# A conv and attention trunk in split fp32: z projected last, products of one width, LayerNorm's channel sums on VectorE

## The chip, the cores and the metric

The kernel runs on one core of a Trainium2 chip. The metric is device time in microseconds. Three runs of the kernel before took 1514.84, 1517.45 and 1518.55 us: median 1517.45 us.

## The reference

The input x has 256 rows (positions) of 2048 channels, all in float32. Two layers follow each other.

Layer 0: `proj = rmsnorm(x) @ w_in` gives three parts a, b, z of 2048 channels each. `u = a * sigmoid(b)`. A causal depthwise convolution of 31 taps over the positions gives c. `cn` is LayerNorm of c over the channels. `y = silu(cn) * silu(z)`, and `x += y @ w_out`.

Layer 1: keys and values of three dilation groups from one normed x, queries of the three groups and a gate z from another, 16 heads of 128 channels. Attention with a relative bias, one softmax over the three groups of a head, times `silu(z)`, then `x += y @ w_out`, and a final RMSNorm.

## The kernel before, in words

**Split products.** Every float32 operand is kept as two float32r parts: hi (rounded) and lo (what is left). A product is hi*hi + hi*lo + lo*hi. Activations lie transposed in `act_a[:, kt, part, :]` (K tile kt of 16, part 0 is hi, 1 is lo, 256 positions). A weight *slab* is 1 MB: 16 K tiles by 128 output columns. SyncE loads it into a ring `raw` (`load_slab`), ScalarE rounds its two halves to `w_hi` (`split_hi`, L257), GpSimd (conv and both output projections) or VectorE (attention) subtracts to get `w_lo` (`split_lo`, L266), and TensorE multiplies (`project`, L280 and L282). In `project` the w_hi tile is multiplied with 512 columns, both parts of the activation side by side, so the bank of PSUM gets hi*hi in its lower and hi*lo in its upper 256 columns; w_lo with part 0 adds 256 columns to the lower ones. To get the result, ScalarE copies the upper half to SBUF (`copy_upper`, L481; `copy_upper_head`, L579) and VectorE adds the lower half (`add_halves`, L712; `head_sum`, L870).

**Conv stage.** One loop over 16 channel tiles; per tile three slabs a, b, z (`CONV`, three raw buffers, six half-slab buffers). VectorE makes u (`glu`, L747), the z gate (L752), and the 31 taps of the tile before (`tap`, L722 to L728, accumulators in PSUM bank 3, two chains joined at L735). All engines run fixed programs in order; semaphores tie them.

**LayerNorm.** When all taps are done, TensorE multiplies a constant 1/2048 matrix with the 16 tiles of `conv` (mean, L1045), VectorE subtracts it (L792), ScalarE squares (L514), TensorE does 16 products again (variance, L1051), ScalarE takes the root (L517), VectorE the reciprocal (L795). Then for each tile: VectorE scales (L802), ScalarE silu with gain and bias (L523), VectorE times the gate (L806), ScalarE rounds to hi (L528), VectorE subtracts to lo (L810). The first product of `a_w_out` (`out_project`, L300 to L302) waits for the lo of tile 0.

**After it.** Four column chunks of `a_w_out` in four slabs each; RMSNorm, transposes, the two inputs of layer 1 (`kv_input`, `q_input`); 16 heads of ten slabs, with the scores, softmax and attention of the head before put between slabs; `b_w_out`; the final norm.

The relative bias rows are made by three products (L1034) after the first three slabs, copied to SBUF (L760) and stored to DRAM by SyncE after the loads of the conv stage.

Of the kernel before, what the change touches and what calls it, by code (L numbers as in the profile page):

```python
# [30 lines left out]
P = 128  # L31
S = 256
# [61 lines left out]
Y_LOOP_SPLITS = {10: (2, (0,)), 13: (2, (1,))}  # L94
LATE_Q_INPUT = {2: range(4, 8), 3: range(8, 12), 4: range(12, KT)}

CONV = Stream(0, 3 * KT, 3, 3, 6, 0)
A_OUT = Stream(3 * KT, CHUNKS * KT // RKT, KT // RKT, 4, 4, 6 * KT)
# [4 lines left out]
def fills(stream, slot):  # L103

    n = 0
    for s in (CONV, A_OUT, QKV, B_OUT):
# [12 lines left out]
def build(nc, x, a_norm, a_w_in, a_conv_w, a_conv_b, a_ln_g, a_ln_b, a_w_out, kv_norm, w_kv, b_norm,  # L119
          b_w_in, b_w_out, rel_bias, final_norm, bucket_rows, out):  # L120
    ctx = ExitStack()
    with ctx:
# [8 lines left out]
        def sem(name):  # L131
# [9 lines left out]
        taps = sb("taps", [P, TAP_ROWS + 1])  # L141
# [12 lines left out]
        upper = sb("upper", [P, 3, S])  # L154

        xn, u, a_sum, b_sum, b_sig, z_sum, z_sig, odd_taps, ln_std, ln_rstd = shared(
            ("xn", [P, TT, D], F32), ("u", [P, TAPS - 1 + S], F32), ("a_sum", [P, S], F32),
            ("b_sum", [P, S], F32), ("b_sig", [P, S], F32), ("z_sum", [P, S], F32),
            ("z_sig", [P, S], F32), ("odd_taps", [P, S], F32), ("ln_std", [P, S], F32),
            ("ln_rstd", [P, S], F32))  # L160
# [18 lines left out]
        bias_vec = raw[0:HEADS, 1, 0:NG * BIAS_W]  # L179
# [17 lines left out]
        upper_copied, summed = sem("upper_copied"), sem("summed")  # L197
        b_gated, z_gated, gate_ready = sem("b_gated"), sem("z_gated"), sem("gate_ready")
        u_ready, taps_copied, tap_done = sem("u_ready"), sem("taps_copied"), sem("tap_done")
        mean_ready, centered, squared, var_part = sem("mean_ready"), sem("centered"), sem("squared"), sem("var_part")  # L200
# [33 lines left out]
        def load_slab(sp, stream, turn, j, src):  # L234

            slot = stream.slot(j)
            if isinstance(turn, int) and turn == 0 and j < stream.ring:
                before = {id(CONV): None, id(A_OUT): CONV, id(QKV): A_OUT, id(B_OUT): QKV}[id(stream)]
# [31 lines left out]
        def project(pe, stream, turn, j, dst, source, source_ready=None):  # L270


            for half in (2 * j, 2 * j + 1):
                slot = stream.half_slot(half)
                pe.wait_ge(lo_dve if stream is QKV else lo_pool, stream.lo_halves(turn, half))
                for k in range(KT // 2):
                    kt = (half % 2) * (KT // 2) + k
                    if source_ready is not None:
                        pe.wait_ge(source_ready, kt + 1)
                    nc.tensor.matmul(dst[:, 0:2 * S], w_hi[:, slot, k * P:(k + 1) * P],  # L280
                                     source[:, kt, :, :], start=(kt == 0), stop=False)
                    mm = nc.tensor.matmul(dst[:, 0:S], w_lo[:, slot, k * P:(k + 1) * P],  # L282
                                          source[:, kt, 0, :], start=False, stop=(kt == KT - 1))
# [67 lines left out]
        def _(sp):  # L351
# [6 lines left out]
            for j in range(3):  # L358
                load_slab(sp, CONV, 0, j, w_in_cols[:, :, j * D:j * D + P])
# [3 lines left out]
            with sp.Fori(1, KT) as c:  # L363
                cols = [sp.snap(c * P + j * D) for j in range(3)]
                for j in range(3):
                    load_slab(sp, CONV, c, j, w_in_cols[:, :, bass.ds(cols[j], P)])

            sp.wait_ge(vec_copied, NG)
            sp.dma_start(bias_dram.ap(), bias_vec).then_inc(vec_stored, 16)
            sp.wait_ge(vec_stored, 16)  # L370
# [51 lines left out]
        def _(pool):  # L422
# [8 lines left out]
            with pool.Fori(0, KT) as c:  # L431
                for j in range(3):
                    split_lo(pool, CONV, c, j, lo_pool)
# [9 lines left out]
        def _(act):  # L443
# [17 lines left out]
            split_hi(act, CONV, 0, 0)  # L461
            act.wait_ge(param_ready, 2)
            for kt in range(KT):
# [5 lines left out]
                if kt in (9, 13):  # L469
                    split_hi(act, CONV, 0, 1, halves=((kt - 9) // 4,))  # L470


            def copy_upper(c, j):


                act.wait_ge(mm_done, CONV.mm_halves(c, 2 * j + 1))
                if j == 0:
                    positive(act, summed, 3 * c - 2)
                else:
                    act.wait_ge(summed, 3 * c + 1)  # L480
                nc.scalar.activation(upper[:, j, :], bank[j][:, S:2 * S], ACT.Copy).then_inc(upper_copied, 1)  # L481
# [710 lines left out]
```

## Time and profile before

The profiled execution took 1517.13 us, its span 1515.3 us.

| | before |
|---|---|
| median of 3 runs | 1517.45 us |
| profiled execution, and its span | 1517.13 us, 1515.3 us |
| TensorE busy | 1462.7 us (97%) |
| VectorE busy | 861.6 us (57%) |
| ScalarE busy | 704.0 us (46%) |
| GpSimd busy | 386.9 us (26%) |

The span starts with the first instruction and ends with the last one. A busy share over the whole span mixes stages; the rows further down are read stage by stage. Starts are in us from the span's start. The time of one instruction of a pipelined engine is longer than the distance to the next one's start; where instructions follow each other it is the distance of the starts that counts.

### The profile page before, as it was taken

The numbers are of one execution on the slowest core, as the hardware profiler recorded it, in microseconds if no ns is written. First come the engines' busy times: TensorE is split into PE (matmuls) and PEld (weight loads), VectorE is DVE, ScalarE is ACT, GpSimd is POOL, SyncE is SP. The second block draws the span as 40 slices with busy tenths as digits, with TensorE's granted clock in tenths as the row PEclk, the third lists the DMA queues.
The fourth block names the chain that finished last, engine by engine and source line by source line (L and its number), as shares of the span: only waits on it lengthen the run. The fifth ranks groups of instructions, "written<-read, shape, count | busy, mean of one in ns | idle before, by whom it ended". The sixth has DMA issues, their size and how long they took to land.

```text
span 1515.3 us, 23156 instructions
## 1 busy us (share of the span) xinstructions
PE 1462.7 (97%) x8198; PEld 1272.7 (84%) x8198; DVE 861.6 (57%) x1433; ACT 704.0 (46%) x1036; POOL 386.9 (26%) x168
## 2 busy tenths in 40 slices
PE   6999999969989999999999999999999999999997
PEld 5888888747868888888888888888888888888786
DVE  3798998971175554555555555555555554554333
ACT  6444444355454444444444444454444444544543
POOL 4888888608800000000000000000000000000595
PEclk9999999979999999999999999999999999999999
DMA  8666666505569656666566666665666656653652
GB/s 224 195 187 187 190 194 192 198 1 173 160 197 255 180 167 179 191 177 177 166 183 184 179 176 172 180 189 162 186 177 180 188 157 186 180 165 118 250 195 83
DMA packets 454127, 268.32 MB, mean 177 GB/s; under 512 B 4353, under 2 KB 436481, under 8 KB 453426
## 3 DMA queue, kind: packets, MB, share of 16 engines
q1 hardware_dynamic: 454098, 267.99, 61.4%
q8 instruction: 14, 0.23, 0.1%
q14 instruction: 9, 0.07, 0.0%
q10 hardware_dynamic: 6, 0.02, 0.0%
HBM read 263.71 MB, written 4.29 MB: 177 GB/s over the span
## 4 chain that ended last, share of the span: by engine, by line
issue 77%; POOL 15%; PE 6%; ACT 1%; DMA 1%; POOLq 0%; DVE 0%; SPq 0%; ACTq 0%
POOL w_lo L266 15%; PE bank L301 2%; PE bank L300 2%; PE bank L302 2%; DMA param_rows<-a_ln_b_dram 1%; ACT act_a L466 0%; ACT w_hi L257 0%; PE bank L1016 0%; POOLq L265 0%; PE bank L1007 0%; SPq L356 0%; ACT bank L654 0%; DVE y L972 0%; POOLq L431 0%; DVE resid L956 0%
## 5 line engine op out<-in xcount | busy, mean ns | idle before, releaser
L280 PE MATMUL bank<-act_a,w_hi 128*128 128x512 f32 x2304 | 807.4, 394 | 6.2 <-DVE k_t L870 3.1
L266 POOL TENSOR_TENSOR w_lo<-raw,w_hi 128x1024 fp32r<-128x1024 f32 x160 | 386.0, 2434 | 1111.9 <-ACT w_hi L257 1111.8
L282 PE MATMUL bank<-act_a,w_lo 128*128 128x256 f32 x2304 | 645.3, 280 | 0.0
L257 ACT ACTIVATE w_hi<-raw 128x1024 fp32r<-128x1024 f32 x480 | 501.7, 1060 | 295.2 <-PE bank L282 217.6
L266 DVE TENSOR_TENSOR w_lo<-raw,w_hi 128x1024 fp32r<-128x1024 f32 x320 | 390.6, 1229 | 281.0 <-ACT w_hi L257 278.5
L280 PEld LDWEIGHTS bank<-act_a,w_hi 128*128 128x128 f32 x2304 | 434.0, 188 | 103.2 <-DVE k_t L870 3.4
L282 PEld LDWEIGHTS bank<-act_a,w_lo 128*128 128x128 f32 x2304 | 434.0, 188 | 0.0
L280 PE MATMUL bank<-act_b,w_hi 128*128 128x512 f32 x1024 | 357.8, 393 | 0.0
L282 PE MATMUL bank<-act_b,w_lo 128*128 128x256 f32 x1024 | 286.3, 280 | 0.0
L280 PEld LDWEIGHTS bank<-act_b,w_hi 128*128 128x128 f32 x1024 | 192.3, 188 | 41.9
L282 PEld LDWEIGHTS bank<-act_b,w_lo 128*128 128x128 f32 x1024 | 192.3, 188 | 0.0
L579 ACT ACTIVATE upper<-bank 128x256 f32<-128x256 f32 x160 | 61.5, 385 | 276.0 <-PE bank L282 276.0
L728 DVE SCALAR_TENSOR_TENSOR bank<-u,taps,bank 128x256 f32<-128x256 f32 x448 | 179.8, 486 | 0.0
L300 PE MATMUL bank<-w_hi,act_a 128*128 128x512 f32 x240 | 96.4, 402 | 7.8 <-DVE act_a L810 5.0
L301 PE MATMUL bank<-w_lo,act_a 128*128 128x512 f32 x240 | 95.6, 398 | 0.0
L302 PE MATMUL bank<-w_hi,act_a 128*128 128x512 f32 x240 | 95.1, 396 | 0.0
L481 ACT ACTIVATE upper<-bank 128x256 f32<-128x256 f32 x48 | 18.5, 386 | 99.2 <-PE bank L282 99.2
L300 PEld LDWEIGHTS bank<-w_hi,act_a 128*128 128x128 f32 x240 | 45.6, 190 | 20.2 <-issue 5.4
L870 DVE TENSOR_TENSOR k_t<-bank,upper 128x256 f32<-128x256 f32 x48 | 20.4, 424 | 62.9 <-PE bank L1080 37.9
L302 PEld LDWEIGHTS bank<-w_hi,act_a 128*128 128x128 f32 x240 | 45.5, 190 | 11.3
L301 PEld LDWEIGHTS bank<-w_lo,act_a 128*128 128x128 f32 x240 | 45.5, 190 | 10.6
L870 DVE TENSOR_TENSOR q_t<-bank,upper 128x256 f32<-128x256 f32 x48 | 20.4, 425 | 49.5 <-ACT upper L579 49.5
(119 smaller groups left out, 717.3 us busy)
## 6 DMA issues: line engine op xcount, KB each, us to landing
raw<-w_kv_dram SPq DMA_DIRECT2D x96, 1024.0 KB, 6.0
raw<-b_w_in_dram SPq DMA_DIRECT2D x64, 1024.0 KB, 6.6
raw<-a_w_in_dram SPq DMA_DIRECT2D x48, 1024.0 KB, 5.8
raw<-a_w_out_dram SPq DMA_DIRECT2D x16, 1024.0 KB, 5.0
raw<-b_w_out_dram SPq DMA_DIRECT2D x16, 1024.0 KB, 5.1
bias<-bias_dram SPq DMA_DIRECT2D x16, 384.0 KB, 8.1
x_sb<-x_dram SPq DMA_DIRECT2D x2, 1024.0 KB, 7.4
resid_dram<-x_sb SPq DMA_DIRECT2D x1, 2048.0 KB, 8.6
```

What stands on the lines that cost most here:

```text
L257: nc.scalar.activation(w_hi[:, stream.half_slot(half), :], raw[:, slot, part:part + HALF], ACT.Copy).then_inc(hi_done, 1)
L266: eng.tensor_tensor(w_lo[:, stream.half_slot(half), :], raw[:, slot, part:part + HALF], w_hi[:, stream.half_slot(half), :].bitcast(F32), A ...
L280: nc.tensor.matmul(dst[:, 0:2 * S], w_hi[:, slot, k * P:(k + 1) * P], source[:, kt, :, :], start=(kt == 0), stop=False)
L282: mm = nc.tensor.matmul(dst[:, 0:S], w_lo[:, slot, k * P:(k + 1) * P], source[:, kt, 0, :], start=False, stop=(kt == KT - 1))
L300: nc.tensor.matmul(banks[t][:, :], y_h, wide_hi, start=(kt == 0), stop=False)
L301: nc.tensor.matmul(banks[t][:, :], y_h, wide_lo, start=False, stop=False)
L302: mm = nc.tensor.matmul(banks[t][:, :], y_l, wide_hi, start=False, stop=(kt == KT - 1))
L481: nc.scalar.activation(upper[:, j, :], bank[j][:, S:2 * S], ACT.Copy).then_inc(upper_copied, 1)
L579: nc.scalar.activation(upper[:, j % 2, :], bank[j % 2][:, S:2 * S], ACT.Copy).then_inc(upper_copied, 1)
L728: nc.vector.scalar_tensor_tensor(out=odd_taps[:, :] if k == TAPS - 2 else acc, in0=u[:, k:k + S], scalar=taps[:, tap_row(k):tap_row(k) + 1 ...
L870: nc.vector.tensor_tensor(dst, bank[j % 2][:, 0:S], upper[:, j % 2, :], ALU.add).then_inc(summed, 1)
```

## The change

- All a and b slabs are projected first: a loop of 8 turns with two tiles each (`AB`, four raw buffers, four half-slab buffers, PSUM banks 0 to 3), then the 16 z slabs (`ZS`, written out, not a loop).
- `project` has three products of 256 columns that all add to the lower 256 columns of the bank: w_hi with part 0, w_hi with part 1, w_lo with part 0. No copy of the upper half and no sum: the sigmoid of b, the silu of z (ScalarE, one `Silu` in place of sigmoid and product) and GLU read PSUM. In the attention part ScalarE copies the 256 columns to k_t, v_t, q_t, z_t (`copy_head`).
- `u` is a ring of four tiles. VectorE's taps run as one sequence of 496: after GLU of tile c it goes on up to tap 26*(c+1), and does the rest after the last GLU. The accumulators move to bank 4, the taps' factors are read from `param` directly.
- After each fourth tile VectorE adds four tiles of `conv` into `ch_sum`; TensorE makes the mean from four products in place of 16, put behind z slab 8. The squares come on ScalarE behind the split of z slab 12, VectorE sums them in fours, the variance product stands behind z slab 11, the root behind the split of slab 14. The reciprocal lies in PSUM. VectorE scales four tiles at a time; all 16 silus come on ScalarE ahead of the first split of `a_w_out`. Then the y products, and the hi and lo parts.
- The bias rows' products come after the first slab, SyncE stores them behind the first four z loads; they lie in `gate`.

```diff
-                    nc.tensor.matmul(dst[:, 0:2 * S], w_hi[:, slot, k * P:(k + 1) * P],
-                                     source[:, kt, :, :], start=(kt == 0), stop=False)
-                    mm = nc.tensor.matmul(dst[:, 0:S], w_lo[:, slot, k * P:(k + 1) * P],
-                                          source[:, kt, 0, :], start=False, stop=(kt == KT - 1))
+                    wide_hi = w_hi[:, slot, k * P:(k + 1) * P]
+                    wide_lo = w_lo[:, slot, k * P:(k + 1) * P]
+                    nc.tensor.matmul(dst[:, 0:S], wide_hi, source[:, kt, 0, :], start=(kt == 0), stop=False)
+                    nc.tensor.matmul(dst[:, 0:S], wide_hi, source[:, kt, 1, :], start=False, stop=False)
+                    mm = nc.tensor.matmul(dst[:, 0:S], wide_lo, source[:, kt, 0, :],
+                                          start=False, stop=(kt == KT - 1))
...
 # ScalarE
+            def gate_b(turn, n):
+                act.wait_ge(mm_done, AB.mm_halves(turn, 4 * n + 3))
+                positive(act, u_ready, 2 * turn + n - 1)
+                nc.scalar.activation(b_sig[:, n, :], bank[2 * n + 1][:, 0:S], ACT.Sigmoid).then_inc(b_gated, 1)
+            with act.Fori(2, KT // 2) as i:
+                for j in range(4):
+                    split_hi(act, AB, i, j)
+                    if j % 2 == 0:
+                        gate_b(i - 1, j // 2)
+            for n in range(KT):
+                split_hi(act, ZS, n // 4, n % 4)
+                if n in (0, 2):
+                    gate_b(KT // 2 - 1, n // 2)
+                if n >= 3:
+                    gate_z(n - 3)
+                if n == SQUARE_SLOT:
+                    for q in range(4):
+                        act.wait_ge(centered, q + 1)
+                        nc.scalar.activation(squares[:, q, :, :], conv[:, 4 * q:4 * q + 4, :],
+                                             ACT.Square).then_inc(squared, 1)
+                if n == STD_SLOT:
+                    act.wait_ge(var_ready, 1)
+                    nc.scalar.activation(ln_std[:, :], bank[7][:, 0:S], ACT.Sqrt,
+                                         bias=eps).then_inc(ln_std_ready, 1)
+            for kt in range(KT):
+                act.wait_ge(ln_scaled, kt // 4 + 1)
+                nc.scalar.activation(conv[:, kt, :], conv[:, kt, :], ACT.Silu, ...)
             split_hi(act, A_OUT, 0, 0)
+            gate_z(KT - 3)
             split_hi(act, A_OUT, 0, 1)
+            gate_z(KT - 2)
+            for kt in range(KT):
+                if kt == 0:
+                    act.wait_ge(mm_done, ZS.mm_halves(KT // 4 - 1, 7))
+                if kt == 2:
+                    gate_z(KT - 1)
+                act.wait_ge(y_ready, kt + 1)
+                nc.scalar.activation(act_a[:, kt, 0, :], conv[:, kt, :], ACT.Copy).then_inc(y_hi, 1)
                 if kt in Y_LOOP_SPLITS:                       # {7: (2, (0,)), 14: (2, (1,))}
                     split_hi(act, A_OUT, 0, *Y_LOOP_SPLITS[kt])
...
 # VectorE
+            for c in range(KT):
+                glu(c)
+                taps_up_to(min((c + 1) * PAIR_TAPS, (c + 1) * TAPS))      # PAIR_TAPS = 26
+            taps_up_to(KT * TAPS)
+            (centring by the mean, four pieces)
+            for q in range(4):
+                dve.wait_ge(squared, q + 1)
+                nc.vector.tensor_reduce(ch_sum[:, q, :], squares[:, q, :, :].rearrange("p k s -> p s k"),
+                                        AX.X, ALU.add).then_inc(sq_summed, 1)
+            (reciprocal, scaling in four pieces)
+            for kt in range(KT - 1):
+                gated_y(kt)
+            for kt in range(KT):
+                dve.wait_ge(y_hi, kt + 1)
+                nc.vector.tensor_tensor(act_a[:, kt, 1, :], conv[:, kt, :], act_a[:, kt, 0, :].bitcast(F32),
+                                        ALU.subtract).then_inc(y_lo, 1)
+                if kt == 4:
+                    gated_y(KT - 1)
...
 # TensorE
+            with pe.Fori(1, KT // 2) as i:
+                for j in range(4):
+                    pe.wait_ge(b_gated if j % 2 else u_ready, 2 * i + (j // 2 - 1))
+                    project(pe, AB, i, j, bank[j], act_a)
+            for n in range(KT):
+                if n < 4:
+                    pe.wait_ge(b_gated if n % 2 else u_ready, KT + (n // 2 - 1))
+                else:
+                    pe.wait_ge(gate_ready, n - 3)
+                project(pe, ZS, n // 4, n % 4, bank[n % 4], act_a)
+                if n == MEAN_SLAB:                            # 8
+                    pe.wait_ge(vec_copied, NG)
+                    for q in range(4):
+                        pe.wait_ge(ch_summed, q + 1)
+                        mm = nc.tensor.matmul(bank[6][:, 0:S], mean_w[:, :], ch_sum[:, q, :], start=(q == 0), stop=(q == 3))
+                    mm.then_inc(mean_ready, 1)
+                if n == VAR_SLAB:                             # 11
+                    for q in range(4):
+                        pe.wait_ge(sq_summed, q + 1)
+                        mm = nc.tensor.matmul(bank[7][:, 0:S], mean_w[:, :], ch_sum[:, q, :], start=(q == 0), stop=(q == 3))
+                    mm.then_inc(var_ready, 1)
...
 # attention, ScalarE (VectorE's head_sum is gone)
+            def copy_head(h, j):
+                dst = [k_t, v_t, q_t][j // NG][:, j % NG, :] if j < 3 * NG else z_t[:, :]
                 act.wait_ge(mm_done, QKV.mm_halves(h, 2 * j + 1))
+                if j == 3 * NG:
+                    act.wait_ge(z_gate_ready, h + 1)
+                nc.scalar.activation(dst, bank[j % 2][:, 0:S], ACT.Copy).then_inc(head_copied, 1)
```

## Rows read from the trace of the kernel before

**Rows 1.** The page: TensorE's busy time, the granted clock in 40 slices, ScalarE's splits.

```profile
PE 1462.7 (97%) x8198; PEld 1272.7 (84%) x8198; DVE 861.6 (57%) x1433; ACT 704.0 (46%) x1036; POOL 386.9 (26%) x168
...
PEclk9999999979999999999999999999999999999999
...
L257 ACT ACTIVATE w_hi<-raw 128x1024 fp32r<-128x1024 f32 x480 | 501.7, 1060 | 295.2 <-PE bank L282 217.6
```

**Rows 2.** A stretch of the attention part: length, busy us by engine, clock.

```profile
600.00:800.00 200.00, 200.00 (x1176) 176.99 (x1175) 107.47 (x133) 90.39 (x129) 0.00 (x0) 1.00 0.63 177
```

**Rows 3.** Timeline of TensorE around LayerNorm: start, us, idle before it.

```profile
296.51 6.74 PE L1045 MATMUL bank<-conv,mean_w 128*128 128x256 f32 x30 [3.56 <-DVE conv L735]
...
328.37 0.77 PE L300 MATMUL bank<-w_hi,act_a 128*128 128x512 f32 x1 [5.00 <-DVE act_a L810]
```

**Rows 4.** Groups of instructions by form: busy us, mean ns, idle before, releasers.

```profile
L300 PE MATMUL bank<-w_hi,act_a 128*128 128x512 f32 x240 | 96.4, 402 | 7.8 <-DVE act_a L810 5.0 <-POOL w_lo L266 2.7
...
L889 DVE TENSOR_REDUCE stat<-prob 128x1 f32<-128x768 f32 x16 | 15.2, 947 | 0.0
```

**Rows 5.** Timelines of ScalarE, VectorE, TensorE at the third attention slab.

```profile
445.33 0.39 ACT L579 ACTIVATE upper<-bank 128x256 f32<-128x256 f32 x1
...
446.93 0.42 DVE L870 TENSOR_TENSOR k_t<-bank,upper 128x256 f32<-128x256 f32 x1
...
447.41 0.50 PE L280 MATMUL bank<-act_a,w_hi 128*128 128x512 f32 x1 [3.06 <-DVE k_t L870]
```

**Rows 6.** Timeline of TensorE: the fourth conv slab's start, and two attention pairs.

```profile
43.09 0.50 PE L280 MATMUL bank<-act_a,w_hi 128*128 128x512 f32 x1
...
700.42 0.39 PE L280 MATMUL bank<-act_a,w_hi 128*128 128x512 f32 x1
700.65 0.28 PE L282 MATMUL bank<-act_a,w_lo 128*128 128x256 f32 x1
700.77 0.39 PE L280 MATMUL bank<-act_a,w_hi 128*128 128x512 f32 x1
```

**Rows 7.** Timeline of TensorE: six fp32 products of 256 columns, six of 128.

```profile
1432.31 1.46 PE L1107 MATMUL bank<-prob_t,v_rows 128*128 128x256 f32 x6
1433.60 0.83 PE L1109 MATMUL bank<-prob_t,v_rows 128*128 128x128 f32 x6
```

**Rows 8.** Timeline of VectorE over one tile of taps.

```profile
150.16 0.55 DVE L722 TENSOR_SCALAR bank<-u,taps 128x256 f32<-128x256 f32 x1
...
156.49 0.41 DVE L712 TENSOR_TENSOR b_sum<-bank,upper 128x256 f32<-128x256 f32 x1
156.82 5.18 DVE L728 SCALAR_TENSOR_TENSOR bank<-u,taps,bank 128x256 f32<-128x256 f32 x13
...
163.37 0.62 DVE L747 TENSOR_TENSOR u<-a_sum,b_sig 128x256 f32<-128x256 f32 x1
163.91 0.41 DVE L712 TENSOR_TENSOR z_sum<-bank,upper 128x256 f32<-128x256 f32 x1
```

**Rows 9.** Timeline of TensorE after that hole: first and last slow wide product.

```profile
448.69 0.63 PE L280 MATMUL bank<-act_a,w_hi 128*128 128x512 f32 x1
...
451.25 0.63 PE L280 MATMUL bank<-act_a,w_hi 128*128 128x512 f32 x1
```

**Rows 10.** Timelines of VectorE and ScalarE in LayerNorm.

```profile
311.44 4.62 DVE L792 TENSOR_TENSOR conv<-conv,bank 128x1024 f32<-128x1024 f32 x4 [0.98 <-PE bank L1045]
...
323.92 1.75 DVE L795 RECIPROCAL ln_rstd<-ln_std 128x256 f32<-128x256 f32 x1 [7.86 <-ACT ln_std L517]
...
312.70 4.45 ACT L514 ACTIVATE xn<-conv 128x1024 f32<-128x1024 f32 x4 [14.99 <-DVE conv L792]
...
323.90 1.28 ACT L523 ACT_TABLE_LOAD   x1
326.16 1.09 ACT L523 ACTIVATE conv<-conv,param 128x256 f32<-128x256 f32 x2 [0.98 <-DVE conv L802]
```

**Rows 11.** Timelines of VectorE (alone, and beside POOL) and of POOL.

```profile
326.80 0.42 DVE L806 TENSOR_TENSOR conv<-conv,gate 128x256 f32<-128x256 f32 x1 [0.33 <-ACT conv L523]
...
338.03 2.24 DVE L806 TENSOR_TENSOR conv<-conv,gate 128x256 f32<-128x256 f32 x1 [0.40 <-ACT conv L523]
...
337.58 2.41 POOL L266 TENSOR_TENSOR w_lo<-raw,w_hi 128x1024 fp32r<-128x1024 f32 x1 [41.11 <-ACT w_hi L257]
```

More of the change, by code:

```diff
@@ L781, in _ @@
-            last = KT - 1
-            load_taps(last, param[:, last, 0:TAP_ROWS + 1])
-            for k in range(TAPS):
-                tap(last, k)
-            join_taps(last, conv[:, last, :])
-            gate_out(last, gate[:, last, :])
+            done_taps = [0]
+            for c in range(KT):
+                glu(c)
+                taps_up_to(min((c + 1) * PAIR_TAPS, (c + 1) * TAPS))
+            taps_up_to(KT * TAPS)
             dve.wait_ge(mean_ready, 1)
             for q in range(4):
-                mean = bank[4][:, 0:S].unsqueeze(1).to_broadcast([P, 4, S])
+                mean = bank[6][:, 0:S].unsqueeze(1).to_broadcast([P, 4, S])
@@ L1025, in _ @@
             pe.wait_ge(in_lo, 2)
-            for j in range(3):
+            for j in range(4):
                 if j == 1:
                     pe.wait_ge(in_lo, KT)
-                project(pe, CONV, 0, j, bank[j], act_a, in_lo if j == 0 else None)
-            pe.wait_ge(bias_in, 32)
-            pe.wait_ge(rel_mask, 1)
-            for g in range(NG):
-                nc.tensor.matmul(bank[5 + g][0:HEADS, :], rel, buckets[:, g * BIAS_W:(g + 1) * BIAS_W],
-                                 start=True, stop=True).then_inc(vec_made, 1)
@@ L1036, in _ @@
-            with pe.Fori(1, KT) as c:
-                for j in range(3):
-                    pe.wait_ge(summed, 3 * c + (j - 2))
-                    project(pe, CONV, c, j, bank[j], act_a)
-            for kt in range(KT):
-                if kt in (0, KT - 1):
-                    pe.wait_ge(tap_done, (TAPS + 1) * (KT - 1 if kt == 0 else KT))
-                mm = nc.tensor.matmul(bank[4][:, 0:S], mean_w[:, :], conv[:, kt, :], start=(kt == 0),
-                                      stop=(kt == KT - 1))
@@ L1047, in _ @@
-            mm.then_inc(mean_ready, 1)
-            for q in range(4):
-                pe.wait_ge(squared, q + 1)
-                for k in range(4):
-                    mm = nc.tensor.matmul(bank[5][:, 0:S], mean_w[:, :], squares[:, q, k, :],
-                                          start=(q + k == 0), stop=(q + k == 6))
-                mm.then_inc(var_part, 1)
+                project(pe, AB, 0, j, bank[j], act_a, in_lo if j == 0 else None)
+                if j == 0:
+                    pe.wait_ge(bias_in, 32)
+                    pe.wait_ge(rel_mask, 1)
+                    pe.wait_ge(in_lo, KT)
+                    for g in range(NG):
+                        if g == 2:
+                            pe.wait_ge(vec_copied, 1)
+                        nc.tensor.matmul(bank[6 + g % 2][0:HEADS, :], rel, buckets[:, g * BIAS_W:(g + 1) * BIAS_W],
+                                         start=True, stop=True).then_inc(vec_made, 1)
```

263 lines of the change are left out of this document (106 added, 157 removed).

## The prediction

> **What bounds the kernel now.** I read the page's busy table and clock line first, then the grouped instructions, then single stretches. TensorE is busy for 97% of the span and its granted clock stands at the upper level except in slices 8 and 9 [rows 1], so the time is the number of columns that it streams plus the holes. In the attention part one slab (16 K tiles of w_hi over 512 columns, w_lo over 256) follows the other with no hole: 200.00 us busy in 200 us [rows 2]. There only the price of the products counts, and an edit on VectorE or ScalarE is worth nothing. The large hole is LayerNorm's: the last conv product ends at 296.51 - 3.56 = 292.95 us (so it starts 0.28 before, and a next one could follow at 292.8), the first product of a_w_out starts at 328.37 [rows 3], 35.6 us later. In between come the taps of the last tile, two sums by ones-matmuls, the centring, squares, root, and the first y. Smaller holes: 2.7 us that products of a_w_out wait for POOL [rows 4], and 3.06 us at the third attention slab, for a sum on VectorE that stands behind its own split and its q inputs [rows 5].
>
> **The product split in three (every slab of a, b, z, q, k, v).** Per K tile 512+256 columns become 256+256+256: the same 768 columns, one matmul and one weight load more. Between starts, the 512-column product takes 230 ns (700.42 to 700.65) and the 256-column one about 120 ns by the two decimals of the rows [rows 6]. More exactly: from 43.09 to 292.8 us run 45 slabs of 16 pairs [rows 3, 6], 5.55 us a slab, 346.8 ns a pair, so 230 + 116.8. Three narrow ones at 116.8 are 350.4 ns: +3.6 ns a K tile, 5.61 us a slab. Does the extra load fit? The load for the next wide product already hides in the 117 ns window, and six fp32 products with a load each follow one another at (0.83 - 0.275)/5 = 111 ns [rows 7]. Lower end: cost goes by columns alone, 347, nothing added. Upper end: the fp32 256-column product, 216 ns ((1.46 - 0.38)/5) [rows 7], which is another data type and far off; I take 353 as the upper end I believe. Accumulating into columns used 117 ns before is not new, the wide product does so now.
> The attention part has 160 slabs, 2560 K tiles, all on the path: 2560 x 3.6 = **+9.2 us** (0 to +16). The same toll of 768 x 3.6 = 2.8 us in the conv part is inside the times below.
> The Trainium skill, "TensorE: Matmul & The Clock Gate" (Wait — 56ns, not 53.3ns?), has a fixed cost of about 2.5 ns per matmul at the full clock beside columns over 2.4 GHz, which speaks against cutting a product in two; by it the toll would be 6.4 us in place of 9.2. The page does not give the trace's price: 512 columns would be 215.8 ns by it and are 230 here.
>
> **Projections in the order a, b, then z.** All tiles now need 32 slabs for a and b. At 43.09 us three slabs and the bias product are behind us [rows 6]; after, slab 1 starts two slabs (11.1) earlier, at 32.0. Slab 31 ends at 32.0 + 31 x 5.61 = 205.9, z slab 8 at 256.4, all of z at 295.7, if nothing waits.
> VectorE per tile now: from 150.16 to 163.91 is 13.75 us [rows 8]; without the sum of b (0.33) and without GLU (0.54), 12.9 for 31 taps and their join. GLU reads its first operand from PSUM now and costs 0.35 like the sums of that form (0.33 from 156.49 to 156.82). So 13.2 us a tile. Its first GLU must wait for a sigmoid that ScalarE issues behind the split of slab 4, which waits for the end of slab 2 (43.2): with the tail of that split (1.06 for a half slab [rows 1], booked as 1.2 with its wait) and the sigmoid (0.4, as the copy of that size in [rows 5]) 44.8 us. In each period of two slabs (11.2) it does one GLU and 26 taps: 0.35 + 26/31 x 12.9 = 11.2. Balanced; the three channel sums that fall inside push it at most 3.6 us, against 3.5 to 4 us of room before the a product of two tiles on is held up. So no stall there, but no slack either.
> Channel sum: four reductions of 1024 elements, strided. From 128x768 in 947 ns [rows 4] about 1.2 us; half as much or twice as much are the ends. VectorE ends its conv work at 44.8 + 16 x 13.2 + 4 x 1.2 = **261** us. TensorE is at that point since 256.4: a new wait of 4.6 us. After the 3.06 us hole TensorE ran at the lower clock (five pairs at 0.64 us against 0.35 [rows 9]), a loss of 1.6; I book 1.7 here too. What else goes from VectorE (the copy of the taps, the sums of a and z, the product of z with its sigmoid) is absent from the 13.2 already; of ScalarE three copies and a sigmoid a tile go and one silu comes, with ScalarE busy for less than half of the span [rows 1]: nothing on the path.
>
> **LayerNorm beside z.** After 261: last mean product 0.6 (three of the four are done in advance), slabs 9 and 10 with the slow clock 12.9 to 274.5; centring 4.6 [rows 10] hides under them. ScalarE reaches the squares behind the split of slab 12 (1.2 after slab 10's end) and a gate (0.4): 276.1; squares 4.5 [rows 10], last reduction 1.2, variance product 0.5: 282.3, a wait of 2.2 for TensorE after slab 11 (280.1). Slabs 12 to 15 end at 304.7. Root (0.5, and a table load), reciprocal 1.75 and scaling (as the centring, 4.6) [rows 10] go under slabs 13 and 14. ScalarE then: split of slab 15 behind slab 13's end (293.5) to 294.7; table load 1.28 and a gate 0.4 to 296.4; sixteen silus at 0.5 (1.09 for two of 0.6) [rows 10] to 304.5; two slabs of a_w_out split with a gate after each: 309.2; first y rounded 309.5.
> Now y_lo. It has two SBUF inputs, and such an instruction waits for a POOL split that is running: 2.24 us in place of 0.42 from 338.03, beside the split of 337.58 to 339.99 [rows 11]. After, POOL splits the first two a_w_out slabs without pause, 305.6 to about 316, and VectorE has y 13 (its gate comes at 306.8), y 14 and y_lo 0 in that stretch. Each gets in once per split: 308.3, 311.0, 313.7. So the first a_w_out product starts at **313.7**, in place of 328.4: **-14.7 us**; TensorE idle 9 us before it, so the slow start of the stage stays as it is now. With both ends: y_lo never held, -18.9; every further y_lo held, -10.
> The Trainium skill, "GPSIMD Engine Reference" (1. Specifications, the line on SBUF interfaces), puts this contention on two SBUF inputs and on fast two-port modes; that would spare the reductions and the scaling (ln_rstd now in PSUM), whose price beside POOL no row shows. Were they held as well, the new wait at 256.4 would grow by some 4 us.
> In the first a_w_out slabs the splits of slab 2 come after y 7 and y 14, so before TensorE needs them (11 us after the start; ready after 8): the 2.7 us behind POOL [rows 4] go. **-2.7 us**.
>
> **Attention.** ScalarE copies each product out of PSUM, VectorE's 160 sums go. Steady state: no hole there before, nothing gained; ScalarE does the same number of copies of the same size. At the third slab TensorE waited until 447.41 for k_t, which VectorE began at 446.93, behind its split and four q inputs; ScalarE's copy is done by 445.72 [rows 5]. That is 1.6 us earlier, and with the hole halved the clock may stay up (1.6 more, half booked): **-2.4 us**. The bias product moved up and the bias store moved beside z: SyncE waits there 5 us at most while four slabs are already loaded; nothing.
>
> **Sum.** -14.7 - 2.7 - 2.4 + 9.2 = -10.6 us. The profiled execution took 1517.13 us (span 1515.3 and 1.8 around it), beside a median of 1517.45; 1517.1 - 10.6 = **1506.5 us**.
>
> **Rivals.**
> (a) VectorE sets the pace of a and b. For: 11.2 us of work in an 11.2 us period; each tile now begins with a wait for the join of the one before. At 0.3 us more a tile the sums end 5 us later, all of it on the path. Against: the same taps run at an even pitch now. 1511 to 1516, say 1513.
> (b) Slower: the repeated load. If a narrow product directly behind a narrow one costs more than 116.8 ns, the attention part pays for it 7680 times. It decides from 118.2 ns on (10.6 / 7680 = 1.4 ns above); at 120 ns it is +24.6 us, 1531. For: no row has two such products in a row. Against: the 111 ns of [rows 7].
> (c) Cheap: products cost by columns (-9.2) and y_lo is not held (-4.2): 1493; with one of the two, 1497 to 1502.
> (d) The change does not do what it says: the hole is only moved, TensorE waits at the mean, the variance and y for as long together as before. I have 4.6 + 2.2 + 9 = 16 us in place of 35.7; with the reductions twice as dear (+4.8 at each of the two) it is 25 and the time 1516.
>
> **Numbers.** Forecast 0.46 (own range 1501 to 1512); (a) 0.16; (b) 0.14; (c) 0.16; (d) 0.08. What this kernel's measurements tell from no change is about 0.3%, 4.5 us. Faster (below 1512.9): nearly all of the forecast and of (c), a third of (a): 0.66. Same: rest of (a), (d), edges: 0.19. Slower: (b) and a little of the rest: 0.15. Eight in ten: 1496 to 1521.
>
> **What would show it.** Slab length in the attention part: 5.61 us right, 5.55 is (c), above 5.68 is (b). In the z stage: TensorE idle 4 to 6 us at the mean product near 256 to 261, 2 at the variance, 9 before the first a_w_out product near 314. POOL's splits and y_lo alternating there. No hole over 2 us at the third attention slab. A TensorE hole at the a product of late tiles is (a). What makes the prediction wrong: a slab price off by 0.05 us (8 us), or a conv end on VectorE later than 266.

## The result, and the profile after

The changed kernel takes 1530.45 us (median of 4 runs, 1529.47 to 1534.64), the kernel before 1516.14 us (4 runs beside them, 1514.48 to 1518.55). The ratio is 1.0098, 95% interval 1.0073 to 1.0124: slower by 1%, where 1506.5 us was forecast. Experiments below that give no number of runs were executed once; the changed kernel itself took 1529.5 to 1536.5 us in five executions, so of single runs the price of a product is compared, and times only where they differ by more. The profiled execution took 1529.53 us with a span of 1527.7 us, so 12.4 us more than before.

The page of the changed kernel, as in [rows 1]: TensorE is still busy for 97%, its granted clock reads 9 in every slice (it was at the lower level for 6.8 us from 316.6, at the wait ahead of `a_w_out`), and its weight loads went from 84% to 94%.

```profile
PE 1484.1 (97%) x11478; PEld 1440.6 (94%) x11478; DVE 797.0 (52%) x1190; ACT 689.1 (45%) x989; POOL 387.0 (25%) x168
...
PEclk9999999999999999999999999999999999999999
```

TensorE's timeline of the changed kernel in the attention part, as in [rows 6]. One K tile is now three starts that lie exactly 0.12 us apart, 0.36 us together, against 0.35 before.

```profile
700.40 0.28 PE L286 MATMUL bank<-act_a,w_hi 128*128 128x256 f32 x1
700.52 0.28 PE L287 MATMUL bank<-act_a,w_hi 128*128 128x256 f32 x1
700.64 0.28 PE L288 MATMUL bank<-act_a,w_lo 128*128 128x256 f32 x1
700.76 0.28 PE L286 MATMUL bank<-act_a,w_hi 128*128 128x256 f32 x1
```

TensorE's timeline around LayerNorm, as in [rows 3]: the wait at the mean is 2.18 us, those at the variance are 0.19, 1.15 and 1.13 us (2.5 together, ahead of its second to fourth product), 7.94 us stay ahead of `a_w_out`, whose first product starts at 319.74 instead of 328.37.

```profile
265.81 0.70 PE L1048 MATMUL bank<-ch_sum,mean_w 128*128 128x256 f32 x2 [2.18 <-DVE ch_sum L772]
...
284.40 0.70 PE L1053 MATMUL bank<-ch_sum,mean_w 128*128 128x256 f32 x2 [0.19 <-DVE ch_sum L800]
...
319.74 0.77 PE L306 MATMUL bank<-w_hi,act_a 128*128 128x512 f32 x1 [7.94 <-DVE act_a L821]
```

VectorE's timeline there, as in [rows 10, 11]: one reduction is 1.93 us; y 13 and y 14 take 1.39 and 1.73 us instead of 0.4, and of the five y_lo's in the last row (6.07 us together) the first two start 2.5 us apart, the others 0.33.

```profile
263.83 1.93 DVE L772 TENSOR_REDUCE ch_sum<-conv 128x256 f32<-128x1024 f32 x1
...
313.22 1.39 DVE L814 TENSOR_TENSOR conv<-conv,gate 128x256 f32<-128x256 f32 x1 [3.29 <-ACT gate L502]
315.38 1.73 DVE L814 TENSOR_TENSOR conv<-conv,gate 128x256 f32<-128x256 f32 x1 [0.77 <-ACT gate L502]
317.03 6.07 DVE L821 TENSOR_TENSOR act_a<-conv,act_a 128x256 fp32r<-128x256 f32 x5
```

The timeline of POOL (GpSimd): four splits without a pause lie beside exactly that stretch.

```profile
311.99 9.83 POOL L270 TENSOR_TENSOR w_lo<-raw,w_hi 128x1024 fp32r<-128x1024 f32 x4 [8.12 <-ACT w_hi L261]
```

At the third attention slab, as in [rows 5], TensorE's product starts at 430.56 after 1.66 us of idle time, where it was 3.06.

Where the time went, between starts on TensorE in the two profiled executions (us):

| stretch | before | after | difference | forecast |
|---|---|---|---|---|
| span's start to first conv product | 22.12 | 21.37 | -0.8 | 0 |
| to first product of `a_w_out` | 306.25 | 298.37 | -7.9 | -14.7 |
| to first attention product | 103.12 | 97.38 | -5.7 | -2.7 |
| to last attention product | 977.76 | 1006.80 | +29.0 | +6.8 |
| to last product | 97.61 | 95.25 | -2.4 | 0 |
| sum | 1506.86 | 1519.17 | +12.3 | -10.6 |

**The measure used below** is the K tile: the length of a whole slab from its first w_lo product to the next slab's, over 16, as a mean over the 100 to 104 slabs of the attention part with nothing in between. It is 346.7 ns before and 359.9 after. (The expectations quote steps within a slab, without the shorter step to the next slab: 348.4 before and 361.5 after, of the same executions.) The windows of 800 to 1200 us show prices by their count of products, the first (x...) of a row: TensorE is busy for all 400 us in each, so between kernels with as many products a K tile more products means cheaper ones. The two rows here, before and after, have two and three products a K tile and can't be compared with each other; they are for the kernels further down.

```profile
800.00:1200.00 400.00, 400.00 (x2356) 354.17 (x2355) 217.31 (x271) 183.63 (x267) 0.00 (x0) 1.00 0.64 179
```

```profile
800.00:1200.00 400.00, 400.00 (x3292) 397.72 (x3291) 187.06 (x202) 178.12 (x258) 0.00 (x0) 1.00 0.62 173
```

### The profile page after: what moved, and what is told of

It reads as the page before. It is cut to its first block, busy times and chain, and to the rows that moved or that the text cites. A ratio compares the mean times of both kernels' runs of the same rounds, so it can differ in the third digit from the quotient of the medians.

```text
span 1527.7 us, 28300 instructions
## 1 busy us (share of the span) xinstructions
PE 1484.1 (97%) x11478; PEld 1440.6 (94%) x11478; DVE 797.0 (52%) x1190; ACT 689.1 (45%) x989; POOL 387.0 (25%) x168
## 4 chain that ended last, share of the span: by engine, by line
issue 76%; POOL 18%; PE 5%; POOLq 0%; DVE 0%; ACT 0%
POOL w_lo L270 18%; PE bank L306 2%; PE bank L308 2%; PE bank L307 2%; POOLq L269 0%; ACT bank L680 0%; DVE y L964 0%; DVE resid L948 0%; PE bank L1108 0%; ACT y L701 0%; PE bank L326 0%; PE bank L325 0%; PE bank L324 0%; PE bank L1110 0%; ACT stat L696 0%
## 5 line engine op out<-in xcount | busy, mean ns | idle before, releaser
L286 PE MATMUL bank<-act_a,w_hi 128*128 128x256 f32 x2304 | 655.6, 285 | 5.3 <-DVE act_b L868 2.4
L288 PE MATMUL bank<-act_a,w_lo 128*128 128x256 f32 x2304 | 652.0, 283 | 0.0
L287 PE MATMUL bank<-act_a,w_hi 128*128 128x256 f32 x2304 | 651.9, 283 | 0.0
L286 PEld LDWEIGHTS bank<-act_a,w_hi 128*128 128x128 f32 x2304 | 442.1, 192 | 7.2 <-DVE act_b L868 2.6
L287 PEld LDWEIGHTS bank<-act_a,w_hi 128*128 128x128 f32 x2304 | 442.3, 192 | 0.1
L288 PEld LDWEIGHTS bank<-act_a,w_lo 128*128 128x128 f32 x2304 | 442.2, 192 | 0.0
L286 PE MATMUL bank<-act_b,w_hi 128*128 128x256 f32 x1024 | 291.0, 284 | 0.0
L287 PE MATMUL bank<-act_b,w_hi 128*128 128x256 f32 x1024 | 289.7, 283 | 0.0
L286 PEld LDWEIGHTS bank<-act_b,w_hi 128*128 128x128 f32 x1024 | 196.5, 192 | 0.0
L287 PEld LDWEIGHTS bank<-act_b,w_hi 128*128 128x128 f32 x1024 | 196.5, 192 | 0.0
L754 DVE SCALAR_TENSOR_TENSOR bank<-u,param,bank 128x256 f32<-128x256 f32 x448 | 179.5, 482 | 0.0
L602 ACT ACTIVATE k_t<-bank 128x256 f32<-128x256 f32 x48 | 18.5, 386 | 112.6 <-PE bank L1081 58.0
L306 PEld LDWEIGHTS bank<-w_hi,act_a 128*128 128x128 f32 x240 | 45.5, 189 | 18.6 <-POOL w_lo L270 9.1
L602 ACT ACTIVATE v_t<-bank 128x256 f32<-128x256 f32 x48 | 18.4, 383 | 87.4 <-PE bank L288 87.4
```

The source lines that it names most:

```text
L286: nc.tensor.matmul(dst[:, 0:S], wide_hi, source[:, kt, 0, :], start=(kt == 0), stop=False)
L287: nc.tensor.matmul(dst[:, 0:S], wide_hi, source[:, kt, 1, :], start=False, stop=False)
L288: mm = nc.tensor.matmul(dst[:, 0:S], wide_lo, source[:, kt, 0, :], start=False, stop=(kt == KT - 1))
L306: nc.tensor.matmul(banks[t][:, :], y_h, wide_hi, start=(kt == 0), stop=False)
L602: nc.scalar.activation(dst, bank[j % 2][:, 0:S], ACT.Copy).then_inc(head_copied, 1)
L754: nc.vector.scalar_tensor_tensor(out=odd_taps[:, :] if k == TAPS - 2 else acc, in0=src, scalar=taps_of[:, tap_row(k):tap_row(k) + 1], in1=acc,
```

## Experiments

### What in the three products costs 13 ns

Four kernels, beside a kernel before of 1515.56 us. The first leaves out half of the hi*lo term.

```diff
-  matmul(dst[:, 0:S], wide_hi, source[:, kt, 1, :], ...)
+  matmul(dst[:, 0:128], wide_hi, source[:, kt, 1, 0:128], ...)      # mid128
```

> The changed kernel, but the middle product of each K tile (w_hi with the lo part) takes 128 columns in place of 256, in all projections. It leaves out half of the hi*lo term. Its own weight load and the next product's stay 128 columns. Theory 'load' (the distance of two products is set by the weight load of the next one, about 120 ns): the distance from the middle product to the third stays 115 to 120 ns, the K tile stays at 355 to 360 ns and the time at 1530. Theory 'columns' (each product pays its columns and a fixed 13 ns): that distance falls to 66 ns, the K tile to 306 ns, and the time by 3328 x 0.053 = 177 us to about 1355.

1506.97 us, K tile 349.0. TensorE's timeline:

```profile
700.62 0.28 PE L286 MATMUL bank<-act_a,w_hi 128*128 128x256 f32 x1
700.73 0.22 PE L287 MATMUL bank<-act_a,w_hi 128*128 128x128 f32 x1
700.79 0.33 PE L288 MATMUL bank<-act_a,w_lo 128*128 128x256 f32 x1
700.96 0.28 PE L286 MATMUL bank<-act_a,w_hi 128*128 128x256 f32 x1
```

The short product is followed after 0.06 us, but the product behind it is recorded 0.05 longer and the next starts 0.17 later. Neither theory is right. The two steps behind the short product take 0.23 us together. The loads go on evenly meanwhile: over 650 to 1200 us their starts lie 109, 119 and 120 ns apart, 116.3 on average, with the short product as with the full ones. That fits a row of loads that sets the pace here, at 116 ns; the 120 ns of the changed kernel lie above it.

```diff
-  matmul(dst[:, 0:S], wide_hi, source[:, kt, 1, :], ...)
+  matmul(dst[0:64, 0:S], wide_hi[:, 0:64], source[:, kt, 1, :], ...)   # stat64: half the outputs of this term left out
```

> The changed kernel, but the middle product of each K tile uses only 64 of the 128 stationary columns (it fills half of the output partitions); the hi*lo term of the other half is left out. So the load ahead of the middle product is half as wide, which runs beside the first product. Theory 'load': the distance from the first to the middle product falls below 120 ns, towards the 106.7 ns that 256 columns take at 2.4 GHz; the other two distances stay at 120; time down by 3328 x 0.013 = up to 44 us. Theory 'columns': all three distances stay at 120 ns, the time at 1530.

1506.89 us, K tile 350.3: with half as wide a second load all three steps are cheaper, not that one alone. The price is not set by one load's length.

```diff
 # apart: kernel before, K tiles 1 to 15 (the upper half keeps its columns)
-  matmul(dst[:, 0:2 * S], w_hi..., source[:, kt, :, :], ...)
+  matmul(dst[:, 0:S], w_hi..., source[:, kt, 0, :], ...)
+  matmul(dst[:, S:2 * S], w_hi..., source[:, kt, 1, :], ...)
```

> The kernel before, with the wide product cut in two of 256 columns for K tiles 1 to 15 of each slab, the second one still into the upper half of the bank: three products and three loads, but no columns are shared by the first two. Theory 'sharing' (the changed kernel pays because three products in a row add to the same columns): 346.8 to 350 ns a K tile, time 1516 to 1528. Theory 'number of products': 360 ns a K tile, 208 slabs x 15 x 13.2 ns = 41 us more, about 1555 (some of it hidden in no place, as TensorE is busy 97%).

1534.34 us, K tile 352.3: cutting the product costs the kernel before 5.6 ns a K tile, 14 us in the attention part. More than the 3.6 forecast, but not 13.2.

```diff
 # wide_att: changed kernel, attention as before (512 + 256, ScalarE copies the upper half, VectorE adds)
+  if stream is QKV: matmul(dst[:, 0:2 * S], wide_hi, source[:, kt, :, :], ...)
```

> The changed kernel with the attention part's products as before: one of 512 and one of 256 columns, ScalarE copies the upper half, VectorE adds the lower. The conv part keeps the three narrow ones and its new order. If the narrow products are the whole loss: 160 slabs x 16 x 13.2 ns = 33.8 us less, plus 1.5 to 3 us lost again at the third attention slab and 0.5 at the last head: 1530.5 - 33.8 + 2.5 = 1499 us, faster than the kernel before by 1.1%. If something else in the new order costs time in the attention part (more work on ScalarE, other waits): above 1508.

1507.35 us (4 runs), ratio to before 0.9945 (0.9929 to 0.9962), K tile 349.7. With the wide product in the attention part the change is worth 8 us; the split of that product is what made it slower. 1499 us was expected: even the wide pair costs 3 ns more than in the kernel before, 7.7 us in 2560 K tiles.

### Columns of PSUM and the order

```diff
 # after_again: the changed kernel as it is
 # after_apart: hi*x_lo goes to the upper columns and stays there (left out of the result)
-  matmul(dst[:, 0:S], wide_hi, source[:, kt, 1, :], ...)
+  matmul(dst[:, S:2 * S], wide_hi, source[:, kt, 1, :], ...)
 # lo_middle: order hi*x_hi, lo*x_hi, hi*x_lo, so that no weights are loaded twice in a row
```

> The changed kernel once more, unaltered, beside the next runs on the same chip. 360.0 ns a K tile in the attention part and 1530 us, if this price belongs to the kernel; nearer to 352 ns and 1510 us, if it belonged to the chip or the execution that it was profiled on.

> The changed kernel, but the product of w_hi with the lo part goes to the upper 256 columns of the bank (K tiles 1 to 15; K tile 0 as one product of 512 columns). Nobody adds the upper half, so the hi*lo term is left out. Same number of products and loads, same columns, same reads. Theory 'sharing' (three products in a row that add to the same PSUM columns hold each other up, 120.0 ns each): K tile 352 ns as in the kernel before with the product cut in two, 3328 x 8 ns = 25 us less, about 1506. Theory 'loads alone': 360 ns and 1530 us, nothing changes.

> The changed kernel with the order of the three products changed: w_hi with the hi part, w_lo with the hi part, w_hi with the lo part. So the same moving operand comes twice in a row in place of the same weights twice in a row. Theory 'sharing': still 360 ns a K tile, 1530 us. Theory 'same weights loaded twice in a row cost more': about 352 ns and 1510 us.

1536.47, 1528.95 and 1531.32 us (before: 1516.23); K tile 359.9, 359.4 and 359.9. Neither the sharing of columns nor the same weights twice costs anything to speak of. after_again has the same K tile and loses its 6 us ahead of the attention part (first `a_w_out` product at 325.74), with a mean granted clock of 0.98 from 20 to 290 us where the first profile had 1.00.

### Where the tensors lie

What was left was that the change dropped the small tensor `taps` (132 bytes, 160 as it is placed) between the weights and the activations, so that `act_a` and `act_b` moved 160 bytes a partition nearer to the weights: `act_a` begins 52736 bytes behind `w_hi`, before it was 52896. No tensor between them was resized, as one of the expectations below has it. An unused tensor moves them back by steps.

```diff
+  gap = sb("gap", [P, 8])          # after_pad32, before_shift; 16: after_pad64
   stat = sb("stat", [P, 32])
```

> The changed kernel with an unused tensor of 32 bytes a partition ahead of stat, so that act_a begins 32 bytes later (at 110240 in place of 110208, as the kernel before begins at 110368; the changed kernel's start is a multiple of 64, these two are not). No instruction changes. Theory 'place' (how the moving operand lies in SBUF sets the price of a 256-column product, 120.0 or 117.4 ns): K tile 352 to 353 ns, 3328 x 7.7 ns = 25 us less, about 1506. Theory 'neighbours' (ScalarE alone reads PSUM now, VectorE does less, and this changes TensorE's pace): 360 ns and 1530.

> The same with 64 bytes: act_a at 110272, again a multiple of 64. If it is the place relative to 64 bytes: 360.0 ns a K tile and 1530 us. If any shift helps: 352 ns and 1506.

> The kernel before with 32 bytes ahead of stat: act_a at 110400, a multiple of 64. Theory 'place': its pair goes from 348.3 ns to about 350.9, 3328 x 2.6 = 8.7 us more, 1524. Theory 'neighbours': 348.3 and 1516.

after_pad32: 1512.00 us (10 runs), ratio 0.9973 (0.9963 to 0.9982) beside a before of 1516.12: an unused tensor takes 18 us off and turns slower into slightly faster. after_pad64: 1522.15 us. before_shift: 1534.28 us; the same 32 bytes cost the kernel before 18 us, twice what was expected, with a K tile of 353.0 in place of 346.7. Windows of after_pad32 and of before_shift:

```profile
800.00:1200.00 400.00, 400.00 (x3379) 397.82 (x3378) 189.22 (x201) 182.60 (x263) 0.00 (x0) 1.00 0.63 177
```

```profile
800.00:1200.00 400.00, 400.00 (x2316) 350.02 (x2315) 214.26 (x269) 180.72 (x261) 0.00 (x0) 1.00 0.62 174
```

Is it the place of the activations or how they stand to the weights, and with what period?

```diff
+  gap_w = sb("gap_w", [P, 8])      # after_all32, before_all32, after_w32
   w_hi = sb("w_hi", ...)
+  gap = sb("gap", [P, 24])         # after_w32, after_pad96; 32: after_pad128, 40: after_pad160
   stat = sb("stat", [P, 32])
```

> The changed kernel with an unused tensor of 96 bytes a partition ahead of the moving operand's tensors, which then begin at 110304 instead of 110208. In 600:1200 us the three distances of a K tile are 120.0 ns each in the changed kernel (360.0 together), 351.7 together at +32 bytes and 354.9 at +64. Theory 'place in 128 bytes': at +96 the sum is again another than 360.0, between 350 and 355, and the time 1510 to 1522 us. Theory 'place in 64 bytes': +96 behaves as +32, 351.7 ns and 1512 us. Theory 'the distance of the weights from the activations grows': the three points have no order, anything from 348 to 360.

> As the run before it with 128 bytes (the tensors begin at 110336). Theory 'place in 128 bytes': back to 120.0 ns each, 360.0 together, 1530 us. Theory 'place in 64 bytes': as at +64, 354.9 ns, 1522 us, and then the 360.0 of +0 must come from something else. Theory 'what else stands at those addresses': not 360.0, no repetition.

> The gap of 32 bytes stands ahead of the weights, so that weights and activations both move by 32 bytes and their distance stays that of the changed kernel. Theory 'the place of the activations alone': as at +32, 351.7 ns and 1512 us. Theory 'how weights and activations stand to each other': as the changed kernel, 360.0 ns and 1530 us.

> Weights moved by 32 bytes, activations by 128. Theory 'the place of the activations alone, in 128 bytes': 360.0 ns and 1530 us. Theory 'how weights and activations stand to each other, in 128 bytes': not 360.0 but as at +96, with the time of that run.

> The changed kernel with an unused tensor of 160 bytes, so that the activations stand 52896 bytes behind the upper weights, as in the kernel before (the change itself brought them 160 bytes nearer, to 52736, by dropping a tensor and shrinking another). Theory 'distance between weights and activations': the three narrow products cost what they cost at this distance in the kernel before with its wide product cut in two, 352.4 ns a K tile (mean over the stage, changed kernel 361.5), and the time is that of the 32-byte shift (351.7 ns, 1512 us) or a little more, 1511 to 1516 us. If something else of the new kernel set the price: 358 to 361.5 ns and 1526 to 1536 us.

> The kernel before with the 32-byte gap ahead of the weights, so weights and activations move together; with the gap between them (before_shift) it took 354.7 ns a K tile and 1534.28 us. Theory 'distance': 348.4 ns and 1516 us, as without a gap. Theory 'absolute place of the activations': 354.7 ns and 1534 us.

after_all32 moves both by 32 bytes: 1534.04 us, K tile 359.9 as without a gap. before_all32 likewise: 1515.03 us and 346.7. The windows of both, beside those of the kernels without a gap above:

```profile
800.00:1200.00 400.00, 400.00 (x3289) 397.61 (x3288) 185.94 (x202) 178.31 (x257) 0.00 (x0) 1.00 0.62 172
```

```profile
800.00:1200.00 400.00, 400.00 (x2356) 354.16 (x2356) 217.82 (x271) 183.74 (x266) 0.00 (x0) 1.00 0.64 179
```

after_w32 (1533.92 us) repeats after_pad96 (1539.24 us): the same distance, both 359.8, where after_pad128 has the activations of after_w32 and 357.2. So it is the distance that counts, not the address. By distance (K tile of the attention part, ns):

| `act_a` minus `w_hi`, bytes | three narrow | wide and narrow |
|---|---|---|
| 52736 | 359.9 (changed kernel, after_all32) | 349.7 (wide_att) |
| 52768 | 350.1 (after_pad32) | 346.8 (wide_att_y_pad32) |
| 52800 | 353.4 (after_pad64) | |
| 52832 | 359.8 (after_pad96, after_w32) | |
| 52864 | 357.2 (after_pad128) | |
| 52896 | 353.7 (after_pad160), 352.3 (apart) | 346.7 (before, before_all32) |
| 52928 | | 353.0 (before_shift) |

No period of 64 or 128 bytes: after_pad128 (1527.76 us) doesn't repeat the changed kernel. after_pad160, at the distance of the kernel before, takes 1520.28 us (5 runs), ratio 1.0040 (1.0026 to 1.0054); its 353.7 is above apart's 352.3, so the expectation of 1511 to 1516 us was too low: the distance is not the whole of the miss.

The table's figures are means, and a mean can hide two prices. In wide_att the pair costs 346.8 with `act_a` and 353.4 with `act_b`, which stands 32768 bytes behind it, from the second head on; in the first head it costs 353 with `act_a` too. TensorE's timeline of wide_att, the first w_lo product of a head's fifth slab and of its sixth (`act_a`), in the first head and in the second: 5.64 us a slab and 5.55, with the same tensors, the same half-slab buffers and the same distance.

```profile
449.62 0.28 PE L292 MATMUL bank<-act_a,w_lo 128*128 128x256 f32 x1
...
455.26 0.28 PE L292 MATMUL bank<-act_a,w_lo 128*128 128x256 f32 x1
...
509.43 0.28 PE L292 MATMUL bank<-act_a,w_lo 128*128 128x256 f32 x1
...
514.98 0.27 PE L292 MATMUL bank<-act_a,w_lo 128*128 128x256 f32 x1
```

after_pad160 has 356 in the conv part up to LayerNorm and with `act_b`, and 352 with `act_a` later on; after_pad32 has 353.3 in the conv part up to LayerNorm and 350.0 behind it. A price mostly holds from slab to slab until other products, a wait or a stretch at the lower clock come between, and from the second head on wide_att and wide_att_y, two executions, have the same prices slab for slab; in the first head they differ (353 and 347). So at one distance more than one price is possible. What picks one is not shown.

### A better version

wide_att with the first half slab of `a_w_out` split before the last silus, the first y's and y_lo's ahead of the other splits:

```diff
 # wide_att_y, ScalarE; VectorE makes the last three y's between y_lo's
+                if kt == 2: split_hi(act, A_OUT, 0, 0, halves=(0,))        # among the silus
...
+                if kt == 1: split_hi(act, A_OUT, 0, 0, halves=(1,)); gate_z(KT - 1)
+                if kt == 3: split_hi(act, A_OUT, 0, 1)                     # among the y_hi's
```

> The kernel with the wide products in the attention part (1507.4 us) and another order around the first product of a_w_out: ScalarE splits the first half slab behind silu 2, the second behind y 1, the next slab behind y 3; VectorE makes y 13 to 15 behind the lo parts 4 to 6. So the first lo parts find no split of POOL in their way. If the 8 us hole of TensorE before a_w_out is POOL's splits holding VectorE (the y_lo product waits for a running split) and ScalarE's four splits ahead of the first y: hole 1.5 to 3 us, time 1507.4 - 5.5 = 1502, and the first slab may wait 1 to 2 us for weights. If the hole is set by the silus alone: 6 to 8 us still, and 1507.

> The kernel with wide products in the attention part and the new y order (1503.3 us), act_a 32 bytes later. Theory 'place': the pair of attention goes from 350.9 ns to the 348.3 of the kernel before, 2560 x 2.6 = 6.7 us, and the conv part's three products from 360 to 352, 768 x 7.7 = 5.9 us of which the a and b part is now near VectorE's pace: 1491 to 1496. Theory 'neighbours': 1503.

1503.30 us (4 runs), ratio 0.9907 (0.9891 to 0.9924) to before; with the gap of 32 bytes 1502.12 us, 0.9906 (0.9889 to 0.9922). Both beat both kernels. In TensorE's timeline of wide_att_y the first `a_w_out` product starts at 316.95 after a wait of 1.54 us in place of 7.94; four more waits of 0.6 to 1.1 us follow it. The gap of 32 bytes gains nothing that the runs could tell.

The gap shortens the attention part by 7 us here (982.1 to 975.1) and most of the conv part's K tiles from 360.0 to 350.0, but the wait at the mean grows from 2.2 to 5.3 us, as VectorE still sets the end of its sums (267.9 and 266.3 us), and `a_w_out` is dearer by 2 us: "place" (1491 to 1496) fell short.

## Why the prediction was wrong

- **The step that failed** is "Three narrow ones at 116.8 are 350.4 ns: +3.6 ns a K tile". In the changed kernel a K tile is 359.9 ns, +13.2, in 2560 K tiles 33.8 us in place of 9.2; that is rival (b) with its 120 ns and its 1531. The 116.8 came from a product that follows a wide one, in a kernel whose activations stand at a favourable distance. The runs part the 13.2 in two: at the distance of the kernel before the three narrow products cost 353.7 against 346.7, +7.0 (cutting the product alone, apart, 5.6); the move by 160 bytes adds 6.2. At 52768 bytes the cut costs 3.3 ns, and the 350.4 of the forecast is met by 350.1: the step was right for one distance and taken for a constant. The upper end of 353 ("as the upper end I believe") rested on no row.
- **Why (b) had too little weight.** That the extra load fits was held from the 111 ns of [rows 7]. Those rows are misread: attention has three fp32 products of each width (L1107, L1109), and the trace shows each as two matmuls, with a load each. So 111 ns is the distance of two such halves of 128 columns, and an fp32 product of 256 columns takes two times 216 ns. What the row does show, loads 111 ns apart, holds, and mid128 has them at 116. But the price rises all the same, with loads that fill 397.7 of 400 us. By the Trainium skill, "TensorE: Matmul & The Clock Gate" (Wait — 56ns, not 53.3ns?), three such products would take an estimated 327.5 ns; the trace has 350 to 360.
- **Conv part and LayerNorm**, -7.9 in place of -14.7. The first `a_w_out` product starts at 319.74, 6.0 us later than the forecast 313.7 (6.8 from the first conv product). The same 360 ns makes a slab 5.76 us and z slab 8 ends at 262.2, not 256.4. Up to the mean that costs nothing: VectorE ends its sums at 265.8, not 261, since a strided reduction takes 1.93 us or a little more in place of 1.2 (2.9 us of the 4.8), and TensorE waits 2.18 us for it in place of 4.6. So 4.6 us are lost there, by VectorE. Slabs 9 to 11 take 17.5 us instead of 18.5, as the booked stretch at the lower clock didn't come. The variance takes 4.8 us of TensorE's time in place of 2.2: the sum booked only the last of the four reductions behind the squares, but at 1.9 us they are slower than the squares and follow each other for 7.7 us. That is the mechanism of rival (d), at part of its size. Slabs 12 to 15 add 0.7 at 360 ns, and y gives 0.8 back. Rival (a) didn't come: no idle time at an a product.
- **y and POOL**: right. The first `a_w_out` product follows the last z product after 8.2 us (9 forecast), and y 13, y 14 and the first y_lo start at 313.22, 315.38 and 317.03, each ending 0.3 us behind a POOL split of 2.4 us. This agrees with the Trainium skill, "GPSIMD Engine Reference" (1. Specifications), on instructions with two SBUF inputs. wide_att_y moves ScalarE's splits and that work at once, and the wait falls to 1.54; the two are not tried apart. By the timelines ScalarE's four splits hold back the first hi part until 315.18, 3.7 us behind the last z product, and VectorE beside POOL takes the rest.
- **`a_w_out`**: -5.7 against -2.7. The waits for POOL went as forecast. The rest, and the -2.4 behind the attention part, has the same cause as the miss with the other sign. In TensorE's timelines of `b_w_out` the first of three products starts at 1479.79 and again at 1480.49 before, at 1479.96 and 1480.64 after: three products with the weights as the moving side take 700 ns before and 680 after, 128 times in each of the two stages, 2.6 us each. It is 680 in after_all32 and 702 to 703 in after_pad96 and after_w32: the distance again.
- **Third attention slab**: k_t's copy starts at 430.11 and the wait is 1.66; 1.4 us less idle and no slow stretch behind it (1.6), 3 us against 2.4. With these, 33.8 us of toll would leave 30.8; the profile of before also has the granted clock at 0.50 for 3.4 us from 431.3, in the first attention slab (1.7 us), and that of after at 1.00 there, which leaves 29.1 beside the measured 29.0. The profile of after_pad32 has such a stretch again, so it is not a lasting gain of the change.
- **The clock row** of before has one slice below 9, the ninth, not two; nothing hangs on it.

**What stays open** is how the distance acts. That reads of weights and activations meet in SBUF would fit stat64 (a smaller load makes all three products cheaper) and the smaller effect on the wide pair, but no run shows it; and two prices at one distance say that the distance is not all of it. Nor was it tried whether `act_b` or `w_lo` matter by themselves, as they moved with the others.

## What to carry over

Where one kind of product fills the span, 1 ns a K tile is 2.6 us: a price that no row shows needs an upper end from a row, and a try of that product alone before the large change. A change that removes or resizes a tensor moves all behind it; compare addresses before blaming the edit, and try one or two unused gaps of 32 bytes when tuning (18 us in the changed kernel, nothing to speak of in wide_att_y). Test a large change in parts: here it held -8 us and +23 us, and only the first was wanted.

## What the runs showed of the hardware

- The price of an fp32r product with 256 columns is 116.7 to 120.0 ns (a third of the K tile) in the attention part, by the distance between stationary and moving operand in SBUF. 32 bytes changed the whole kernel's time by 18 us, in either direction.
- With the same tensors a K tile can stand at either of two prices for many slabs: 346.8 or 353 (wide_att), 350.0 or 353.3 (after_pad32), 352 or 356 ns (after_pad160).
- A short product does not shorten the row: behind one of 128 columns (0.06 us) the next is held, and both steps together take 0.23 us (mid128); loads start 116 ns apart there.
- An fp32 product is two matmuls in the trace, each with its load: with 256 columns 216 ns each, with 128 columns 111.
- A reduction of 1024 elements to 256 with a strided read takes 1.93 us on VectorE, 1.9 ns an element; 768 contiguous ones take 0.95, 1.2 ns an element.
